# High and low weight parts at a chunk pitch of 1056 bytes instead of 1024, in a float32 transformer kernel on one core

## The reference, cut to what matters

```python
proj = h @ w_in[l]                                   # 1024 -> 5120 columns, per layer
x = x + mixed @ w_out[l]
up = h @ w_up                                        # 1024 -> 5632
(jax.nn.silu(a) * bval) @ w_down                     # 2816 -> 1024
proj = jnp.einsum("bsd,de->bse", h, w_in)            # the hybrid layer's own
u = jax.nn.relu(jnp.einsum("bsd,df->bsf", m, w_ff1))
x = x + jnp.einsum("bsf,fd->bsd", u * u, w_ff2)
```

## Time and profile before

| | us |
|---|---|
| median of 3 runs | 1054.52 (1054.43 to 1056.76) |
| the profiled execution | 1053.14 |
| its span in the trace | 1051.3 |
| PE busy | 1038.7 (99%) |
| DVE busy | 719.9 (68%) |
| ACT busy | 574.1 (55%) |
| POOL busy | 287.2 (27%) |

### The profile page before, as it was taken

One profiled execution on the slowest core, in us unless ns is written; L12 is line 12 of the kernel. 1 busy time (PEld: TensorE's weight loads), 2 busy tenths in 40 slices (PEclk: granted clock), 3 DMA queues, 4 the chain that ended last, 5 costly groups with the idle time before them and its releaser, 6 DMA issues.

```text
span 1051.3 us, 20017 instructions
## 1 busy us (share of the span) xinstructions
PE 1038.7 (99%) x8398; PEld 984.1 (94%) x8398; DVE 719.9 (68%) x1217; ACT 574.1 (55%) x791; POOL 287.2 (27%) x179
## 2 busy tenths in 40 slices
PE   8999999999999999999999999999999999999997
PEld 7999998999999899999999989998999999899996
DVE  5762248787688775322788967877888789666663
ACT  6454466655355644445765544556658875343443
POOL 0376675100000137666740000013400035001120
PEclk9999999999999999999999999999999999999999
DMA  9644454465763664344455566456432157664841
GB/s 308 202 158 154 157 166 161 161 215 159 228 200 126 208 224 164 124 158 140 156 186 189 173 225 215 133 152 220 122 114 89 61 181 230 191 210 131 261 160 40
DMA packets 169705, 180.11 MB, mean 171 GB/s; under 512 B 4240, under 2 KB 166416, under 8 KB 169488
## 3 DMA queue, kind: packets, MB, share of 16 engines
q1 hardware_dynamic: 169616, 178.84, 52.8%
HBM read 177.78 MB, written 1.05 MB: 170 GB/s over the span
## 4 chain that ended last, share of the span: by engine, by line
PE 84%; DVE 8%; ACT 4%; POOL 2%; issue 1%; DMA 1%; SPq 0%; POOLq 0%; ACTq 0%; DVEq 0%
PE psum L679 83%; DVE sb_w_lo L1861 3%; POOL sb_w_lo L2615 1%; ACT sb_scratch L1329 1%; ACT sb_w_hi L1329 1%; DVE psum L1845 1%; DVE sb_xg_lo L1845 1%; POOL sb_scratch L2655 1%; DVE sb_scratch L1845 1%; DMA sb_raw<-in_w_in 1%; PE psum L906 1%; DVE sb_xt L1879 0%; DVE sb_xt L1877 0%; ACT L1329 0%; DVE sb_hid_both L1936 0%
## 5 line engine op out<-in xcount | busy, mean ns | idle before, releaser
L1329 ACT ACTIVATE sb_w_hi<-sb_raw 128x2048 fp32r<-128x2048 f32 (+3 forms) x185 | 318.7, 1727 | 162.0 <-PE psum L679 98.6
L679 PE MATMUL psum<-sb_xg_hi,sb_w_hi 128*128 128x256 f32 x1656 | 401.8, 283 | 0.4 <-DVE psum L1845 0.3
L679 PE MATMUL psum<-sb_xg_lo,sb_w_hi 128*128 128x256 f32 x1656 | 396.7, 279 | 0.0
L1861 DVE TENSOR_TENSOR sb_w_lo<-sb_raw,sb_w_hi 128x2048 fp32r<-128x2048 f32 (+3 forms) x150 | 305.9, 2042 | 104.4 <-ACT sb_w_hi L1329 103.3
L679 PEld LDWEIGHTS psum<-sb_xg_hi,sb_w_hi 128*128 128x128 f32 x1656 | 310.2, 187 | 3.7 <-issue 0.9
L679 PEld LDWEIGHTS psum<-sb_xg_lo,sb_w_hi 128*128 128x128 f32 x1656 | 310.7, 188 | 0.3
L679 PE MATMUL psum<-sb_xg_hi,sb_w_lo 128*128 128x256 f32 x1656 | 228.4, 280 | 1.0 <-DVE sb_w_lo L1861 0.9
L679 PE MATMUL psum<-sb_hid_both,sb_w_hi 128*128 128x512 f32 (+1 forms) x912 | 210.4, 364 | 0.7 <-DVE sb_hid_both L1936 0.4
L679 PEld LDWEIGHTS psum<-sb_xg_hi,sb_w_lo 128*128 128x128 f32 x1656 | 207.9, 187 | 2.0 <-DVE sb_w_lo L1861 1.4
L2615 POOL TENSOR_TENSOR sb_w_lo<-sb_raw,sb_w_hi 128x2048 fp32r<-128x2048 f32 (+1 forms) x34 | 156.0, 4594 | 107.3 <-ACT sb_w_hi L1329 97.9
L679 PEld LDWEIGHTS psum<-sb_hid_both,sb_w_hi 128*128 128x128 f32 x912 | 148.7, 188 | 22.2 <-DVE sb_hid_both L1936 1.2
(11 more groups left out here) (172 smaller groups left out, 988.4 us busy)
## 6 DMA issues: line engine op xcount, KB each, us to landing
sb_raw<-in_w_in SPq DMA_DIRECT2D x51, 1024.0 KB, 5.2
sb_raw<-in_w_up SPq DMA_DIRECT2D x44, 1024.0 KB, 5.1
sb_raw<-in_w_ff SPq DMA_DIRECT2D x21, 1024.0 KB, 5.6
sb_raw<-in_w_down SPq DMA_DIRECT2D x16, 768.0 KB, 4.9
sb_raw<-in_w_down SPq DMA_DIRECT2D x16, 640.0 KB, 4.4
sb_raw<-in_w_out SPq DMA_DIRECT2D x8, 1024.0 KB, 5.2
sb_raw<-in_w_ff SPq DMA_DIRECT2D x8, 768.0 KB, 4.6
sb_raw<-in_w_ff SPq DMA_DIRECT2D x8, 640.0 KB, 4.5
```

The lines of the kernel that those rows point to most:

```text
L679: return nc.tensor.matmul(ps, lhsT, rhs, start=start, stop=stop, skip_group_check=True)
L1329: return nc.scalar.activation(out_, in_, func, **kw)
L1861: v.tensor_tensor(part(w_lo, s), part(raw, s), part(w_hi, s).bitcast(F32), ALU.subtract)\
```

## The change

`w_hi` and `w_lo` are no longer one buffer of three slots each, but three buffers each. In slabs of 256 columns the chunks lie `PITCH` = 264 elements (1056 bytes) apart; slabs with other column counts keep their chunks end to end. Gaps of 32 bytes lie ahead of the second and the third buffer, and the third begins 16 bytes in. The slots of `w_hi` then begin, by remainder of 1024, at 352, 640 and 944, those of `w_lo` at 192, 480 and 784. With a step of 32 bytes from chunk to chunk the distances take nearly all multiples of 16. `raw` stays as it was; the copies and subtractions now read 8 pieces of 256 (or 6, 5, 4) from `raw` end to end and write them at the new pitch. The instructions of every engine, their order and their waits are the same as before; addresses and the shapes of these access patterns alone differ.

```diff
+PITCH = 264
...
+        def slots(name, before, inside):
+            bufs = []
+            for i, (gap, shift) in enumerate(zip(before, inside)):
+                if gap:
+                    sb(f"before_{name}{i}", gap)
+                bufs.append(sb(f"{name}{i}", shift + KD * PITCH, F32R)[:, shift:])
+            return bufs
+
         raw = sb("raw", SLOTS * SLAB)
-        w_hi = sb("w_hi", SLOTS * SLAB, F32R)
-        w_lo = sb("w_lo", SLOTS * SLAB, F32R)
+        w_hi = slots("w_hi", (0, 8, 8), (0, 0, 4))
+        w_lo = slots("w_lo", (0, 8, 8), (0, 0, 4))
...
-        def part(buf, s):
+        def loaded(s):
             i = s.n % SLOTS
-            return buf[:, i * SLAB:i * SLAB + s.chunks * s.cols]
+            return raw[:, i * SLAB:i * SLAB + s.chunks * s.cols].rearrange("p (k c) -> p k c", k=s.chunks)
...
-        def by_chunk(buf, s):
-            return part(buf, s).rearrange("p (k c) -> p k c", k=s.chunks)
+        def by_chunk(bufs, s):
+
+            pitch = PITCH if s.cols == 256 else s.cols
+            return bufs[s.n % SLOTS][:, 0:s.chunks * pitch].rearrange("p (k c) -> p k c", k=s.chunks)[:, :, 0:s.cols]
...
-                f(part(w_hi, s), part(raw, s), ACT.Copy).then_inc(S["split_hi"], 1)
+                f(by_chunk(w_hi, s), loaded(s), ACT.Copy).then_inc(S["split_hi"], 1)
...
-                v.tensor_tensor(part(w_lo, s), part(raw, s), part(w_hi, s).bitcast(F32), ALU.subtract)\
+                v.tensor_tensor(by_chunk(w_lo, s), loaded(s), by_chunk(w_hi, s).bitcast(F32), ALU.subtract)\
                     .then_inc(S["split_lo"], 1)
...
-                        g.tensor_tensor(part(w_lo, s), part(raw, s), part(w_hi, s).bitcast(F32), ALU.subtract)\
+                        g.tensor_tensor(by_chunk(w_lo, s), loaded(s), by_chunk(w_hi, s).bitcast(F32), ALU.subtract)\
                             .then_inc(S["pool_lo"], 1)
```

More of the change, by code:

```diff
@@ L639, in _ @@
             for name, chunks in (("load_half", slice(0, KD // 2)), ("slab_in0", slice(KD // 2, KD))):
-                eng.dma_start(by_chunk(raw, s)[:, chunks, :], s.src.rearrange("(k p) c -> p k c", p=P)[:, chunks, :])\
+                eng.dma_start(loaded(s)[:, chunks, :], s.src.rearrange("(k p) c -> p k c", p=P)[:, chunks, :])\
                     .then_inc(S[name], 16)
@@ L647, in _ @@
                         eng.wait_ge(S[name], value)
-                eng.dma_start(by_chunk(raw, s), s.src.rearrange("(k p) c -> p k c", p=P))\
+                eng.dma_start(loaded(s), s.src.rearrange("(k p) c -> p k c", p=P))\
                     .then_inc(S[f"slab_in{s.n % SLOTS}"], 16)
@@ L817, in raw_chunk @@
                     t = s.tiles[j]
-                    mm = mul(main_bank(t), by_chunk(raw, s)[:, k, j * P:j * P + P], tl(xg_full, k),
+                    mm = mul(main_bank(t), loaded(s)[:, k, j * P:j * P + P], tl(xg_full, k),
                              k == 0 and plan.at[t][1] == 0, k == KD - 1)
@@ L1854, in split @@
                 if s.halved:
-                    hi, lo, whole = by_chunk(w_hi, s), by_chunk(w_lo, s), by_chunk(raw, s)
+                    hi, lo, whole = by_chunk(w_hi, s), by_chunk(w_lo, s), loaded(s)
                     for j in range(2):
```

## The result

The changed kernel takes **1060.7 us** (median of four runs, 1060.0 to 1061.4), the kernel before in the same session 1055.4 (1054.4 to 1056.8). The ratio is 1.0052, with a 95% interval of 1.0038 to 1.0066: slower by some 5.5 us. The forecast was 1054.5 and no difference. The time lies within the range, in the rival *Slower rhythm*.

A forecast was written before the change was run, and what follows sets the result against it. The prediction took PE's stream of matmuls as the bound and summed its three parts as 0 + 0 + 0, staying at the median of the kernel before, 1054.5 us; the range ran from 1046 to 1065.

The forecast's parts named there:

- Slower rhythm: Rival: some new distances make weight loads late in up and input projections, PE waits; 8.4 us more, 1063; chance 0.17.
- What bounds the kernel: Whole kernel: a stream of matmuls on PE, busy 99%; 7944 units at 116.7 ns make 927 us of 1051.3.
- Part 1: Distances between weight load and moving operand in PE's matmuls: taken as 0 us, bounds -79.4 and +8.4 us.
- first place in part 1: Last down projection, 512 columns: half as many loads per column, other distances, yet the same 116.7 ns per 256 columns.
- Part 2: Copies and subtractions of 184 slabs written in pieces on DVE, ACT, POOL: 0 us, at most +9 us on the chain.
- Part 3: Order, waits, transfers and raw unchanged: 0 us; should PE stream faster, DVE would still cover a gain up to 18%.
- Collision undone: Rival: the 24 lost cycles per matmul are a collision at the old remainder, mostly avoided by spreading; -79.4 us at most; chance 0.18.
- Pieces cost on ACT: Rival: each piece costs ACT its fixed part anew, so copies of 8 x 256 lengthen; +9 us, 1064; chance 0.04.
- It does not do what it says: Rival: memory divided in 16-byte units makes new distances act as the old; 1054.5 us; chance within the forecast's 0.61.

The follow-up runs named there:

- e4_worst: The kernel before with w_hi and w_lo both 32 bytes further (d = 32), pitch still 1024: 1068.5 us, ratio 1.0131.
- e5_d108: The kernel before with w_hi and w_lo 108 bytes further by remainder of 256, through padding inside the buffers: 1039.5 us, ratio 0.9858.
- b2_fine: Matmul streams alone, computation left out: distances 4 bytes apart, both operands moved, chunks twice, 512 columns, pitch 1152; d = 60, 64, 68 take 133.3 ns, the fast ones 113.4.
- b1_sweep: Matmul streams alone, computation left out, constant distances in steps of 16 bytes, also 8-column loads and pitch 1056: 113.4 to 120.0 ns per full-width matmul.
- e3_best: The kernel before with w_hi and w_lo both 96 bytes further (d = 96), pitch still 1024: 1047.4 us, ratio 0.9934.
- b3_tiles: Matmul streams alone in the kernel's tile order, 64 distances in steps of 4 bytes, every sixteenth byte again: d = 96 113.3 ns twice, d = 176 119.9 then 116.7.
- e1_pitch: The changed kernel with the pitch of 1056 bytes but without the gaps and the third slot's 16 bytes: 1061.0 us, ratio 1.0059 to the kernel before.
- e6_d120: The kernel before with w_hi and w_lo at d = 120 through padding inside the buffers: 1049.0 us, ratio 0.9946, runs between 1040.8 and 1054.3.

## Why the prediction was wrong

**What bounds the kernel: right.** PE's stream, its interval read from starts, and the count of matmuls held; 206 tiles times the change of one tile gives 7.2 us, where the two traces have 7.5 on all full-width matmuls of 256 columns, and comes within 2 us of the results of e4_worst and e5_d108.

**Part 1, taken as 0 us: this step failed.** At the full clock it was 7.5 us more on 256 columns and 0.7 less on 512 in the profiled pair, and the medians moved by 5.3. It rested on "rows 6 and rows 5 are nearest to the point: other distances, same rate". Neither is near.

- The earlier trace rows are 512 columns wide and at d = 64. In b2_fine such streams take 233.2 ns at d = 0 and 233.2 at d = 64, but 226.65 at 16 and 32: the row compared two entries that happen to be equal. Where the distance was another one, in e4_worst, the last down projection did move, to 226.9.
- The earlier trace rows have loads of 8 columns. b1_sweep has those at 113.3 ns at d = 0 and 128 alike, where full-width loads differ by 2 ns, and in e3_best "ba" itself runs at 113.3. Its 117.0 was one of two rates, near that of the full-width tiles by chance, and told nothing of loads of 128.

The step named its own weak point ("if full-width loads behave otherwise than the short ones of 'ba'"), and that is what the runs found. The row to go by was the one set aside: "v", full-width loads, 256 columns moving, another distance, 118.1 ns. The upper bound made from it, 8.4 us on 5984 matmuls, is close to the 7.5 of the traces, but by luck: the distance of "v", 800, is d = 64 modulo 256, 118.35 in the first sweep, and this one value lies near what the sixteen values of the changed kernel come to, 117.8 by the table and 118.1 measured.

The argument of the first place in part 1 had a fault of logic too. Half as many loads with the same loss per column spoke against the load as the cause of the whole loss, not of a part. The sweep gives the sizes: at 2.4 GHz an interval of 116.7 ns is 280 cycles for 256 columns, one of 113.3 is 272. Of the 24 lost cycles **16 stay** with loads of 8 columns and at the best distance, and **8** are the distance's., 117.9 ns at the old remainders, were rightly read as a rhythm that the distance does not set: d = 0 has 117.95 in b2_fine and 117.8 in the second pass of b3_tiles. That was evidence for several rhythms, not for the distance being harmless.

The Trainium skill (SBUF — State Buffer, section Who interferes with whom) gives PE independent read ports for moving operand and weight load, by which the distance would be worth 0. The trace disagrees: nothing but the addresses changes between the 113.4 and the 120.0 ns of b1_sweep, with no other engine at work. The 262 cycles for 256 columns that the Trainium skill (TensorE: Matmul & The Clock Gate, section Back-to-back issue gap) lists were reached in none of the streams; the lowest is 272.

**Part 2, pieces, 0 us: right.** ACT 1911 ns against 1912, DVE 2311 against 2318, POOL 4737 against 4732.

**Part 3, nothing else: right for the change.** No wait appeared. Its remark that a gain of up to 18% would still be covered was read from one stretch, 300 to 326, and holds there; over the kernel it doesn't: with a 3% faster stream in e5_d108 some 4 to 5 us went into pauses, waits for DVE of up to 1.6 us among them.

**The rivals.** *Slower rhythm* is what happened, with its price (1063 against 1060.7) and its condition (intervals above 117.2: 118.1). Of its signs one came otherwise: the slower tiles are in all three slots, not in one. That the weight load comes late, as the rival says, isn't shown: the records of the loads are as long as before, 188 ns. *Collision undone* had part of the mechanism: there is a loss that the distance sets. It was wrong in that the old distance, d = 0, at 116.7, is among the better of sixteen (mean 118.04), so that spreading moves away from a good value; and in its price, since 8 cycles of 24 can be had, not all. *Pieces cost on ACT* fell: its copy takes 1911 ns. *It does not do what it says*, with units of 16 bytes, fell: in b1_sweep multiples of 16 differ by up to 6.6 ns, in b2_fine steps of 4 bytes do too.

**What stays open.** Why just these distances are slow (a collision in memory is the obvious reading, and no run shows it), why two or three rhythms exist at one distance, which start leads into which, and what sets the rate of "ba". With a pitch of 1056 the first sweep has 117.5 where the tiles of e1_pitch have 118.4 in both parts; b2_fine, each chunk twice as in a tile's high part, has 118.4 and 118.5, but the low part uses each chunk once, so the pattern of reuse can't be all of it.

## What to carry to other kernels

Before an address layout is spread, measure the constant layouts: if the old value is better than the mean of all, spreading is likely to lose, and one well-chosen constant offset (here 108 bytes of padding, nothing else) gains. A rate borrowed from another place of the trace counts only if both operands of the collision have the same shape there; a row that is insensitive by its shape looks just like a row that shows no effect. And a rate that was found in a bare stream has to be confirmed in the kernel with several runs, since one distance can have several rhythms. And before a difference of some us between two traces is explained, look at the granted clock of each stretch: here one short stretch at the lower clock made up 1.5 of 7.6 us.

## What the runs showed of the hardware

- The interval of full-width float32r matmuls of 256 columns depends on the distance between weight load and moving operand, modulo 256 bytes, and down to steps of 4 bytes: 113.3 to 120.0 ns at most distances, up to 123 at a few in b3_tiles and 133.3 at three in b2_fine.
- With weight loads of 8 columns a bare stream takes 113.3 ns at d = 0 and 128, so that 16 cycles more than 256 columns need at 2.4 GHz (106.7 ns) stay. In the kernel such matmuls ran at 117.0 (before) and 113.3 (e3_best).
- At one distance several rates are possible (d = 96: 113.3 and 117.7 to 117.9; d = 64: 118.35 and 133.3; d = 176: 120.0 and 116.7; d = 0: 116.7 and 117.95). In e3_best an unbroken run of tiles keeps the rhythm in which it begins; in e6_d120 the executions of one kernel lie up to 13 us apart.
- The mean duration of a matmul's record moved from 283 to 284 ns when its rate went from 116.7 to 118.1; only the starts show it.
- The granted clock can fall to its lower level for some microseconds in the middle of a dense stream (854.6 to 858.0 us in the changed kernel), with intervals of 213 ns in place of 116 to 119.
